# Narrow projections with one 512-column product for the weights' high part, the bank's halves added by VectorE, and two more low parts by adding transfers

## The reference

```
h = rmsnorm(x, norm_w[l])
proj = einsum('bld,dn->bln', h, w_in[l])
(gdn_qkv, gdn_b, gdn_a, gdn_z, hg_q, hg_f, hg_i, hg_g, s5_u, s5_z,
 ret_q, ret_k, ret_v, ret_g, gate_logits) = split(proj)
y_a = gdn_branch(...);  y_b = hgrn2_branch(...)
y_c = s5_branch(...);   y_d = retention_branch(...)
branch = einsum('blcw,cwd->blcd', stack(y_a, y_b, y_c, y_d), w_branch[l])
merged = sum over branches of sigmoid(gate_logits) * branch
x = x + einsum('bld,de->ble', merged, w_out[l])
```

## Time and profile before

| | us |
|---|---|
| median of 3 runs | 2917.91 (2917.57 to 2918.38) |
| profiled execution, its own time | 2917.88 |
| its span, first to last instruction | 2916.0 |
| PE busy | 2869.0 (98%) |
| PE weight loads busy | 2562.9 (88%) |
| DVE busy | 1977.4 (68%) |
| ACT busy | 1574.0 (54%) |
| POOL busy | 422.3 (14%) |
| chain that ended last, share of PE and of "issue" | 65%, 26% |

### The profile page before, as it was taken

The page is one execution under the profiler, slowest core; times in us unless marked ns, Lnnn a source line. Parts: engine busy times, 40 slices in busy tenths (PEclk is TensorE's granted clock), DMA queues, the critical chain, the costliest instruction groups (busy, mean ns, idle before and its releaser), DMA issues.

```text
span 2916.0 us, 46745 instructions
## 1 busy us (share of the span) xinstructions
PE 2869.0 (98%) x17852; PEld 2562.9 (88%) x17852; DVE 1977.4 (68%) x3177; ACT 1574.0 (54%) x2401; POOL 422.3 (14%) x637
## 2 busy tenths in 40 slices
PE   7999999999999999999999999999999999999998
PEld 6899999999998888888889999999999888888887
DVE  6887788778875555555567877788778755555554
ACT  6556665666564444444556556655665644444443
POOL 3223132213200000000011332123211000000000
PEclk9999999999999999999999999999999999999999
DMA  6676677677766666666656766676667666666655
GB/s 163 163 172 166 175 181 174 164 177 179 175 175 195 194 194 195 193 192 185 192 129 165 178 171 174 172 179 171 171 171 181 181 195 195 192 192 195 194 180 166
DMA packets 636367, 521.56 MB, mean 179 GB/s; under 512 B 26480, under 2 KB 504496, under 8 KB 635760
## 3 DMA queue, kind: packets, MB, share of 16 engines
q1 hardware_dynamic: 612944, 483.46, 59.1%
q0 software_dynamic: 22816, 34.00, 6.8%
q10 hardware_dynamic: 384, 1.11, 0.1%
HBM read 487.02 MB, written 2.10 MB: 168 GB/s over the span
## 4 chain that ended last, share of the span: by engine, by line
PE 65%; issue 26%; DVE 4%; ACT 2%; DVEq 1%; POOL 1%; DMA 1%; ACTq 0%; POOLq 0%
PE PJ L1794 42%; PE S L1794 16%; PE RA L1794 3%; PE GB L1794 2%; DVE mix L1367 1%; DVE w_lo L1223 1%; POOL gnorm L585 0%; POOL w_lo L500 0%; DVE region L1402 0%; ACT w_lo L649 0%; DVE region L1404 0%; DVE region L1405 0%; DVEq L1406 0%; DVE region L1412 0%; DVEq L1413 0%
## 5 line engine op out<-in xcount | busy, mean ns | idle before, releaser
L1223 DVE TENSOR_TENSOR w_lo<-raw_w,w_hi 128x1024 fp32r<-128x1024 f32 (+1 forms) x912 | 1055.3, 1160 | 757.3 <-ACT w_hi L651 729.9
L651 ACT ACTIVATE w_hi<-raw_w 128x1024 fp32r<-128x1024 f32 x912 | 962.5, 1058 | 791.4 <-PE PJ L1794 342.5
L1794 PE MATMUL PJ<-h_hi,w_hi 128*128 128x256 f32 x2560 | 744.7, 291 | 1.6 <-DMA w_lo<-raw_w 1.6
L1794 PE MATMUL PJ<-h_hi,w_lo 128*128 128x256 f32 x2560 | 724.5, 283 | 0.0
L1794 PE MATMUL PJ<-h_lo,w_hi 128*128 128x256 f32 x2560 | 724.3, 283 | 0.0
L1794 PEld LDWEIGHTS PJ<-h_hi,w_hi 128*128 128x128 f32 x2560 | 490.4, 192 | 9.7 <-issue 6.8
L1794 PEld LDWEIGHTS PJ<-h_lo,w_hi 128*128 128x128 f32 x2560 | 490.6, 192 | 0.0
L1794 PEld LDWEIGHTS PJ<-h_hi,w_lo 128*128 128x128 f32 x2560 | 489.9, 191 | 0.0
L1794 PE MATMUL PJ<-w_hi,h_hi 128*128 128x512 f32 x1152 | 461.5, 401 | 1.9 <-DVE h_lo L1698 1.9
L1794 PE MATMUL PJ<-w_hi,h_lo 128*128 128x512 f32 x1152 | 450.4, 391 | 0.0
L1794 PE MATMUL PJ<-w_lo,h_hi 128*128 128x512 f32 x1152 | 449.9, 391 | 0.0
(11 more groups left out here) (386 smaller groups left out, 3988.6 us busy)
## 6 DMA issues: line engine op xcount, KB each, us to landing
raw_w<-w_in SPq DMA_DIRECT2D x576, 512.0 KB, 3.9
raw_w<-w_in SPq DMA_DIRECT2D x512, 128.0 KB, 2.7
raw_w<-w_branch SPq DMA_DIRECT2D x128, 512.0 KB, 4.2
raw_w<-w_out SPq DMA_DIRECT2D x64, 512.0 KB, 4.1
w_lo<-raw_w POOLq DMA_DIRECT2D x112, 256.0 KB, 4.3
raw_w<-s_glu_w SPq DMA_DIRECT2D x16, 512.0 KB, 4.5
ret_decay<-c_ret POOLq DMA_DIRECT2D x16, 128.0 KB, 3.8
out<-x_tok SPq DMA_DIRECT2D x4, 512.0 KB, 4.0
```

Source lines behind the costliest of these rows:

```text
L651: A_(w_hi[i % RING][:, :, :], raw_w[i % RING][:, :, :], ACT.Copy).then_inc(hi_ready, 1)
L1223: TT(w_lo[i % RING][:, 0:ks, :], raw_w[i % RING][:, 0:ks, :], w_hi[i % RING][:, 0:ks, :].bitcast(f32), ALU.subtract).then_inc(raw_used[i % ...
L1794: return nc.tensor.matmul(o, w, m, start=start, stop=stop)
```

## The change

1. h_hi and h_lo become the two parts of one tensor h_parts, so that for a block of weights both lie in 512 columns behind each other. A narrow step is then two products: w_hi by both parts (512 columns, into the whole bank), and w_lo by h_hi (256 columns, into its first half).
2. The two halves of the bank must be added. DVE does it with a reduction (`sum_parts(b)`), ten in a unit, and writes the sum where ACT used to put it; it waits for the block's last half, frees the bank, and signals `summed`. ACT waits for `summed` where it waited for PE; it no longer copies u, the convolution inputs and the rope operands from the bank, and reads the rest from SBUF.
3. DVE's step `ahead(3)` now stands ahead of `conv_taps(0)`, and `ahead(5)` ahead of `conv_taps(1)`.
4. DMA_LOW has two more halves, 12 and 14, both joint. POOL's code is the same, so their transfers are started with those above 10.

```diff
--- before.py
+++ after.py
@@ -45,6 +45,7 @@
 (B_SU, B_GK, B_GQ, B_HF, B_HQ, B_GV, B_RQ, B_RK, B_RG, B_SZ) = range(10)
+NARROW = B_SZ + 1
@@ -54,7 +55,7 @@
-DMA_LOW = (6, 8, 10, 16, 18, 20, 22)
+DMA_LOW = (6, 8, 10, 12, 14, 16, 18, 20, 22)
 OWN = HALF // 2
@@ -192,7 +193,8 @@
-        h_hi, h_lo = sb("h_hi", [P, KT, SEQ], f32r), sb("h_lo", [P, KT, SEQ], f32r)
+        h_parts = sb("h_parts", [P, KT, 2, SEQ], f32r)
+        h_hi, h_lo = h_parts[:, :, 0, :], h_parts[:, :, 1, :]
         raw_w = [sb(f"raw_w{s}", [P, HALF, P]) for s in range(RING)]
...
@@ -762,9 +759,8 @@
-                        src = projected(b)
-                        A_(conv_in[m][:, CONV - 1:], src, ACT.Copy)
-                        A_((gk, gq, gv)[m], src, ACT.Copy, scale=tap(m, CONV - 1)).then_inc(pj_read, 1)
+                        act.wait_ge(summed, n * NARROW + (b + 1))
+                        A_((gk, gq, gv)[m], conv_in[m][:, CONV - 1:], ACT.Copy, scale=tap(m, CONV - 1))
@@ -812,10 +808,9 @@
-                        src = projected(b)
-                        A_(rx[m][:, :], src, ACT.Copy)
-                        A_(rsw[m][0:64, :], src[64:128, :], ACT.Copy)
-                        A_(rsw[m][64:128, :], src[0:64, :], ACT.Copy).then_inc(pj_read, 1)
+                        act.wait_ge(summed, n * NARROW + (b + 1))
+                        A_(rsw[m][0:64, :], rx[m][64:128, :], ACT.Copy)
+                        A_(rsw[m][64:128, :], rx[m][0:64, :], ACT.Copy)
                         act.drain().then_inc(rope_staged, 1)
@@ -823,15 +818,8 @@
-                    def stage_u():
-
-                        act.wait_ge(s5_used, n1)
-                        A_(s_u[:, :], projected(B_SU), ACT.Copy).then_inc(pj_read, 1)
-                        act.drain().then_inc(u_staged, 1)
-
                     ahead(0)
                     if u == 0:
-                        stage_u()
                         ahead(1)
@@ -878,7 +865,8 @@
-                    A_(hsig[:, 0, :], projected(B_HF), ACT.Tanh, scale=0.5).then_inc(pj_read, 1)
+                    act.wait_ge(summed, n * NARROW + (B_HF + 1))
+                    A_(hsig[:, 0, :], hsig[:, 0, :], ACT.Tanh, scale=0.5)
                     act.drain()
@@ -894,7 +882,8 @@
-                    A_(hq[:, :], projected(B_HQ), ACT.Silu).then_inc(pj_read, 1)
+                    act.wait_ge(summed, n * NARROW + (B_HQ + 1))
+                    A_(hq[:, :], hq[:, :], ACT.Silu)
                     act.drain().then_inc(hq_staged, 1)
@@ -951,7 +940,8 @@
                     act.drain().then_inc(g_ms_ready, 1)
-                    A_(gate_of(3), projected(B_RG), ACT.Silu).then_inc(pj_read, 1)
+                    act.wait_ge(summed, n * NARROW + (B_RG + 1))
+                    A_(gate_of(3), gate_of(3), ACT.Silu)
                     act.drain().then_inc(rz_staged, 1)
@@ -959,8 +949,8 @@
                         cosines()
-                    A_(zs[:, ds(u, 1), :].rearrange("p a n -> p (a n)"), projected(B_SZ), ACT.Silu).then_inc(
-                        pj_read, 1)
+                    act.wait_ge(summed, n * NARROW + (B_SZ + 1))
+                    A_(zs[:, u, :], zs[:, u, :], ACT.Silu)
                     ahead(27)
@@ -1360,6 +1350,15 @@
+                    def sum_parts(b):
+
+                        dve.wait_ge(split_used, s0 + (block_slot(b) + 2 + RING))
+                        to = (s_u, conv_in[0][:, CONV - 1:], conv_in[1][:, CONV - 1:], hsig[:, 0, :], hq,
+                              conv_in[2][:, CONV - 1:], rx[0][:, :], rx[1][:, :], yT[:, 3, u, :], zs[:, u, :])[b]
+                        nc.vector.tensor_reduce(to, PJ[b % 2][:, :].rearrange("p (a n) -> p n a", a=2),
+                                                mybir.AxisListType.X, ALU.add).then_inc(pj_read, 1)
+                        dve.drain().then_inc(summed, 1)
+
                     def conv_taps(m):
@@ -1469,6 +1468,7 @@
                             s5_ratio()
+                        sum_parts(B_SU)
                         ahead(1)
@@ -1480,14 +1480,16 @@
                         ahead(2)
+                        sum_parts(B_GK)
                         gate_columns()
+                        ahead(3)
                         conv_taps(0)
-                        ahead(3)
                         if n:
...
                         ahead(4)
+                        sum_parts(B_GQ)
+                        ahead(5)
                         conv_taps(1)
-                        ahead(5)
                         if n:
@@ -1505,13 +1508,15 @@
                         s5_add(0)
+                        sum_parts(B_GK)
+                        ahead(3)
                         conv_taps(0)
-                        ahead(3)
                         ahead(4)
                         s5_turn(1)
-                        conv_taps(1)
+                        sum_parts(B_GQ)
                         ret_finish(u - 1)
                         ahead(5)
+                        conv_taps(1)
                         s5_add(1)
@@ -1520,6 +1525,8 @@
+                    dve.wait_ge(hgrn_used, n1)
+                    sum_parts(B_HF)
                     dve.wait_ge(gnorm_ready, n1)
@@ -1556,10 +1563,12 @@
                         s5_scan(0)
+                        sum_parts(B_HQ)
                         ahead(9)
...
+                        sum_parts(B_GV)
                         dve.wait_ge(hq_staged, n1)
@@ -1621,6 +1633,7 @@
                     s5_back(4)
+                    sum_parts(B_RQ)
                     ahead(21)
@@ -1637,6 +1650,7 @@
                     s5_back(5)
+                    sum_parts(B_RK)
                     ahead(23)
@@ -1652,6 +1666,7 @@
                     dve.drain().then_inc(s5_used, 1)
+                    sum_parts(B_RG)
                     ahead(25)
@@ -1662,6 +1677,7 @@
                     ahead(26)
+                    sum_parts(B_SZ)
                     ahead(27)
@@ -1885,9 +1901,10 @@
                                 pe.wait_ge(h_ready, x0 + (h * HALF + k) // 2 + 1)
-                            last = three_pass(o[:, 0:SEQ], lambda k: (w_hi[i % RING][:, k, :], w_lo[i % RING][:, k, :]),
-                                              k, lambda k: (h_hi[:, h * HALF + k, :], h_lo[:, h * HALF + k, :]),
-                                              h == 0 and k == 0, h == 1 and k == HALF - 1)
+                            at = h * HALF + k
+                            MM(o[:, :], w_hi[i % RING][:, k, :], h_parts[:, at, :, :].rearrange("p a n -> p (a n)"),
+                               at == 0, False)
+                            last = MM(o[:, 0:SEQ], w_lo[i % RING][:, k, :], h_hi[:, at, :], False, at == KT - 1)
                         last.then_inc(split_used, 1)
@@ -1942,7 +1959,7 @@
                         if n:
-                            pe.wait_ge(sa_r, sa0 + 3)
+                            pe.wait_ge(sa_r, sa0 + 4)
                         for a in range(2):
@@ -2021,7 +2038,7 @@
-                        pe.wait_ge(u_staged, n1)
+                        pe.wait_ge(summed, n * NARROW + 1)
                         pe.wait_ge(sa_r, sa0 + (2 + half))
```

More of the change, by code:

```diff
@@ L374, in trunk_kernel @@
         g_ready, gc_written, cols_ready = sem("g_ready"), sem("gc_written"), sem("cols_ready")
-        pj_read = sem("pj_read")
+        pj_read, summed = sem("pj_read"), sem("summed")
         ga_w, ga_r = sem("ga_written"), sem("ga_read")
@@ L391, in trunk_kernel @@
         rope_staged, roped, ret_used = sem("rope_staged"), sem("roped"), sem("ret_used")
-        u_staged, s5_used = sem("u_staged"), sem("s5_used")
+        s5_used = sem("s5_used")
         phase_rounded, phase_ready, sincos_ready, x_re_im_ready = (
```

3 lines of the change are left out of this document (removed).

## The result

The changed kernel takes 3234.85 us (median of 4 runs, 3233.55 to 3235.38), beside 2917.94 us for the kernel before (2917.57 to 2918.38) on the same chip. The ratio is 1.1085, with a 95% interval of 1.1066 to 1.1105: 317 us slower. The forecast was 3225 us, with a range of 3080 to 3290.

The account below looks back on a forecast made before the run. TensorE's own instructions were taken to bound a unit (97.46 of 97.6 us). To the span of 2916.0 us came 229 for thirteen units, 13 for the last, 30 for each layer's first and 37 for clock: forecast 3225, range 3080 to 3290.

Parts of the forecast that it names:

- clock: Behind TensorE's waits at half 12 and in the tail: half clock, some 2.5 us a unit, 37 us in all.
- products: Narrow steps of the projection: one 512- and one 256-column product save 12.5 ns a step, 32 us over 2560 steps.
- The first wait: At the norms: ACT and DVE wait for each other twice, so the squares come 6.8 us later than before.
- The second wait: In joint half 12: w_lo's transfer stands behind the S5 matrices on POOL's queue, so PE waits 8.0 us.
- the sum of v's bank comes about 5 us earlier: At joint half 12: DVE's sum, behind a scan and low part 13, ends about 5 us before w_lo's transfer lands.
- The last unit: No S5 matrices to make; it waits for v's sum instead, 4.6 us less than other units, 13 us longer.
- The third wait: In the tail, sums for RQ and RK delay rope and scores: PE waits 4.0 us, net +3.2 a unit.
- Rival 2: DVE's reduction takes 1.23 us, 0.55 more at four sums, 2.2 us a unit: 3260 us, chance 0.12.
- Rival 1: Only POOL's queue shows, ACT and DVE keep the norms in time: 8.9 us in 15 units, 3044 us, chance 0.14.
- rival 3: Transfers land in time, only ACT and DVE make waits, 9.6 us in 14 units: 3096 us, chance 0.08.
- Rival 4: Waits stay below 2.0 us a unit and PE stays the bound: faster, 2886 us, chance 0.03.
- The place before the next turn: Between the scores and the next S5 turn: 0.3 us less a unit.

Follow-up runs that it names:

- run 1: The kernel before with only the new form of the narrow products, nothing summed and one product left out of the result: 2906.82 us, ratio 0.996.
- Run 4: The changed kernel with DVE's old order at the two convolutions, taps ahead of `ahead(3)` and `ahead(5)`: 3168.58 us, ratio 1.0854.
- run 5: The changed kernel with 28 unused products of 512 columns put ahead of TensorE's wait for the norms: 3223.29 us, ratio 1.1046.
- run 2: The kernel before with only halves 12 and 14 added to the list of low parts by transfer: 3042.49 us, ratio 1.0425.
- run 10: The changed kernel with run 9's three repairs, and the sum of RK's bank moved ahead of the S5 piece: 3090.31 us, ratio 1.0584.
- run 3: The changed kernel with the old list of transfers, so DVE subtracts halves 12 and 14 whole: 3205.86 us, ratio 1.0986.
- run 9: The changed kernel with DVE's taps first again, v's sum ahead of the second scan, and the old list of transfers: 3120.77 us, ratio 1.0696.

## Why the prediction was right, and where it wasn't

The time was right within 10 us, and so was the sum over a unit: 20.6 us more, forecast 20.1. The three places and the chains to the first and the third were right. Taken over the whole execution, though, three terms are off and cancel, and that part is luck. (The 112 is what is left of the busy time; it holds whatever else makes products slow.)

| term | forecast | measured |
|---|---|---|
| idle time of TensorE | +304 (272 over the units, and the 32 of the products in it) | +217 |
| clock | +37 | +112 (100 more busy, though the form takes 12 away) |
| products | -32 | -12 (busy 2857.0 in run 1) |
| sum, span against span | +309 | +317 |

- *The products.* The term was mis-sized: 12.5 ns a step forecast, 4.3 ns measured (11 us over 2560 steps, run 1). The pitch of a 512-column product was read where its neighbours have 512 columns too (226.7 ns); between 256-column products it is 233 ns. That explains 4 of the 8 ns; where the rest goes is open. The sum that the Trainium skill's fixed cost gave ("TensorE: Matmul & The Clock Gate", section "Wait — 56ns, not 53.3ns?": 6.4 us) lies nearer to the result, for no reason of its own: the 512-column product takes 20 ns above its columns here (233 against 213.3), not 2.5.
- *The first wait.* Right: 22.55 us from the turn to the norms, 22.35 forecast; a wait of 7.4 us, 7 forecast. Run 4 shows its cause (ACT and DVE wait for each other by turns), run 5 how little a wait's half clock adds here. In the first unit of each layer there is none (0.03 and 0.47 us), as the forecast had it.
- *The second wait.* Its end was right (24.0 us behind the norms, 24.7 forecast), its cause only half. POOL's queue does what was said (run 2; issue 18.45 us behind gnorm in the changed kernel). But the step "the sum of v's bank comes about 5 us earlier" failed: it ends 1.2 us before the landing in this unit, and behind it in some others. It is also wanted at the fourth product and not at the seventh, which the walk left out. The half clock behind the norms explains only a part. With the clock at 1.00 there (run 5) the sum ends 19.8 us behind the norms, as my walk had it, but the landing comes sooner as well, 22.1 us behind them (334.24 by POOL's next issue, norms at 312.13), so that 2.4 us lie between the two, not 5. Why POOL needs 17.07 us to its issue there, and 18.45 and 18.98 elsewhere, no run shows. The two ends lie close together, so that neither edit alone removes the wait (32 and 41 us are left of 51); both edits do, and waits elsewhere take their place: 29 us for the transfers, 14 for the sum, 38 for both.
- *The last unit.* It waits for v's sum, as said (2.77 us), but that comes late too: the seventh product stands 23.2 us behind the norms, 0.8 less than in the unit above and not 4.6 less.
- *The third wait.* Right in its chain, a little too long: 2.54 and 0.46 us of wait where I had 4.0, and run 10 shows that the sum of RK is in its chain.
- *The clock.* Too small as a term: 7.9 us at 0.57 behind the first wait, where I had 3.6 at 0.53. The forecast said that this part is hidden by the second wait, and run 5 confirms it but for 1.3 us a unit. The same fact seen from the other side makes the idle term too large: what I had as a wait of 8 us at half 12 is one of 3.07, and much of the rest TensorE spends on slow products.
- *Rivals.* Rival 2 is out (0.69 us a reduction). Rival 1 (only POOL) and rival 3 (only ACT and DVE) are both out, by runs 2 and 3: each mechanism is there alone, with +125 us and +288 us, and together they make +317, less than the sum, since both act on the same place. Rival 4, no wait above 2 us, is out by every list of waits.
- *The place before the next turn.* A unit also loses 1.2 us between the scores and the turn, where I had a gain of 0.3; no run took that apart.

What stays open: why a product of 512 columns takes 6 ns more between shorter ones, where the rest of the 32 us of the products goes, and the 10 us by which run 9 beats the sum of its parts. Most of the loss that is left in run 10 (173 us) was not taken apart either; its largest single wait is that for the squares.

## What to carry to other kernels

Read a pitch among the neighbours that the instruction will have, and price the gain before the waits: here the whole worth of the new form was 11 us, and the waits around the added sums and transfers, with the slow products behind them, cost 328 us, thirty times as much. When an engine has 20% idle time, ask at each new instruction who waits for what is queued behind it; in three places of a unit the reduction of 0.68 us cost nothing that could be measured, in two others 1.5 us each in the mean. When two ends come within a few us of each other, removing one leaves most of the wait under another name, so test both together before a cause is named. A list that looks like a choice of engine can also set an order elsewhere in the code (here that of the products in a joint half); read every place that asks for it.

## What was not expected of the hardware

- A 512-column product of w_hi by both parts, followed by a 256-column one, has a pitch of 233 ns (run 1, median), and the pair 350 ns. Products of 512 columns among their like have 227 ns in the joint halves of the same stage and 226.7 ns behind it (96 in 21.76 us).
- Behind a wait of 2.14 us the granted clock was 0.53 for 3.6 us; behind one of 7.41 us it was 0.57 for 7.9 us, most of them at the 1.2 GHz level. With 28 products put into the wait it stayed at 1.00 (run 5), and a unit was 1.3 us shorter.
- A TENSOR_REDUCE that adds the two halves of a bank, 256 elements apart, takes 0.68 to 0.69 us, as long as a TENSOR_TENSOR that reads 512 elements and writes 512, and longer than one that writes 256 (0.42).
